# Twelve identity products on TensorE ahead of each wait for a tile's normalised rows

## The chip, the cores and the metric

The kernel runs on one core of one Trainium2 chip. The metric is the device time of one launch in microseconds. Before the change three runs took 3201.06, 3203.36 and 3207.66 us; the median is 3203.36 us.

## The reference, cut to what matters

Two blocks follow one another on a sequence of 256 tokens of width 1024, each with two layers. The change touches only the first block. There, in each layer, the token mixers' outputs are normalised head by head and projected, the result is added to the residual, and the new residual is normalised again for the router and the experts:

```python
y = rms_norm(y.reshape(bn, m, N_GROUPS * h, HEAD_DIM), head_g.reshape(N_GROUPS * h, HEAD_DIM))
y = y * head_scale[:, None]
return y.reshape(bn, m, MIX_W) @ w_out
...
x = x + g1 * y_lat
x = x + g2 * expert_choice_ffn(rms_norm(x, norm2_g[l]) * (1.0 + sc2) + sh2,
                               router_w[l], exp_w_gate[l], exp_w_up[l], exp_w_down[l])
```

All data are float32. The first layer also carries 256 context tokens through the same steps; the second carries the latent tokens alone.

## The kernel before

Tokens lie in tiles of 128 rows. The first layer of the first block has four tiles (two of latents, two of context), the second has two: six tiles in all. Everything is laid out by hand, with semaphores between the engines and eight PSUM banks. Each bank use is a unit with a number, and units belong to lanes: banks 0 and 1 are the DENSE lane, 2 to 5 and 6 to 7 serve the attention. `bank_for(lane)` takes the next unit of a lane and, from the ninth use on, waits until that bank's previous content has been read.

In the middle of each layer two programs are interleaved step by step on every engine: `attend()`, which works through the attention jobs of all tiles (scores L921, turned weights L302, values L943), and `fill()`, which does the dense work and ends with `out_tile(t)` for each tile. A table written out by hand says how many steps of `fill()` stand behind each step of `attend()`. What `attend()` does not cover is run alone, so the last tile of each layer has no other work beside it.

`out_tile(t)` on TensorE is a chain through three engines:

1. It waits for `xn_ready`: VectorE squares and sums the tile's mixed rows (L2231, L2232), ScalarE takes the roots (L1430), VectorE the reciprocals (L2235) and the scaled rows (L2239).
2. It turns the 128 x 1024 rows with eight transposes (helper `turn`, L302, 128x128 float32 products against the identity) into two DENSE banks, from which VectorE and ScalarE copy them to `HT`.
3. It multiplies them by the two halves of `w_out` (L981, 32 products of 128x512).
4. VectorE adds the result to the residual (L2256, L2257), ScalarE squares and takes the root (L1474, L1430), VectorE writes the normalised rows (L2261). TensorE waits for that, the second `xn_ready` of the tile.
5. It turns these rows with eight transposes, VectorE (L2265) and ScalarE scale them into `HT`, and TensorE makes the router's logits (L1004, 16 products of 128x16).
6. VectorE and ScalarE make the softmax, and VectorE goes on to the squares of the next tile.

Behind a wait of TensorE stands everything that TensorE has still to do, the attention's steps too. After the last tile come the routing, the gathering of the experts' tokens (L1116) and the loop over the 16 experts (L781), whose weights stream in through a ring of slots: SyncE issues a load (L505) each time a product of TensorE frees a slot.

The lines around the two waits are these:

```python
nc.tensor.wait_ge(sem["xn_ready"], pe.due("xn_ready"))
for j in range(2):
    u = bank_for(DENSE)
    for k in range(4):
        last = turn(U(u)[:, k * P:(k + 1) * P], XN[:, t, (4 * j + k) * P:(4 * j + k + 1) * P])
    last.then_inc(full[u % BANKS], 1)
```

Of the kernel before, what the change touches and what calls it, by code (L numbers as in the profile page):

```python
# [14 lines left out]
P = 128  # L15
# [16 lines left out]
CN = 512  # L32
RING = 6
BANKS = 8
RING_2 = 4
SLOTS_2 = (2, 3, 0, 1)
PRE_SLOTS = [(0, 1, 2, 3), (3, 0, 1, 2)]
EXPERT_SLOTS = [(4, 5, 3, 0, 1, 2), (4, 5, 2, 3, 0, 1)]
PRE_CHUNKS = 19
ALL = tuple(range(BANKS))  # L40
DENSE, RULE, SIDE = (0, 1), (2, 3, 4, 5), (6, 7)
# [18 lines left out]
class Count:  # L60


    def __init__(self, name, eng):
        self.name, self.eng, self.per_turn = name, eng, {}
        self.base, self.local = Counter(), Counter()
        self.turn = None
        self.nth, self.taken = list(range(BANKS)), Counter()

# [8 lines left out]
    def unit(self, k=1, lane=ALL):  # L77

        for _ in range(k):
            b = lane[self.taken[lane] % len(lane)]  # L80
            self.taken[lane] += 1
            n = self.nth[b]
            self.nth[b] += BANKS
        return n

    def uses(self, n):

        v = n // BANKS + 1
        return v if self.turn is None else self.turn * (self.per_turn["unit"] // BANKS) + v

# [115 lines left out]
def build(nc, A, out, gate_scratch, band):  # L206
    with ExitStack() as ctx:
        ring = ctx.enter_context(nc.sbuf_tensor("ring", [P, RING * KT * CN], F32))
        arena = ctx.enter_context(nc.sbuf_tensor("arena", [P, ARENA], F32))
        bank = [ctx.enter_context(nc.psum_tensor(f"bank{b}", [P, CN], F32)) for b in range(BANKS)]  # L210
        names = [f"bank_full{b}" for b in range(BANKS)] + [f"bank_free{b}" for b in range(BANKS)]
# [11 lines left out]
        def view(at, width):  # L223
            return arena[:, at:at + width]

        ident, ones = view(0, 128), view(128, 4)
# [4 lines left out]
        U = lambda n: bank[n % BANKS]  # L231
# [28 lines left out]

        X1 = ring[:, RING_2 * KT * CN:RING * KT * CN]
        QKT = [X1[:, 2048 * i:2048 * i + 2048].rearrange("p (b n) -> p b n", b=4) for i in range(2)]
# [34 lines left out]
        mm = nc.tensor.matmul  # L297

        def turn(o, i):

            k = i.shape[0]
            return nc.tensor.transpose(o, i, ident[0:k, 0:k])  # L302
# [126 lines left out]
        def tiles(l):  # L429
            return range(4) if l < DEPTH - 1 else range(2)  # L430
# [51 lines left out]
        def _(eng):  # L482
            count = [0]

            def pre_load(l, *pieces):
# [3 lines left out]
                count[0] += 1  # L489
                if i >= RING_2:  # L490
                    nc.sync.wait_ge(sem["chunk_used"], i - RING_2 + 1)
                elif j == 1:
                    eng.dma_start(X[:, 0:2, :], A["x"][0].rearrange("(t p) n -> p t n", p=P)).then_inc(sem["tokens_in"], 16)
                    eng.dma_start(X[:, 2:4, :], A["ctx"][0].rearrange("(t p) n -> p t n", p=P)).then_inc(sem["tokens_in"], 16)
                    nc.sync.wait_ge(sem["rows_in"], sp.due("rows_in", 16 * 9))
                s = PRE_SLOTS[l][j % RING_2]
                for src, to, n in pieces:
# [39 lines left out]
            def load_2(src, kt=KT, n=CN):  # L537

                q = count[0]
                count[0] += 1  # L540
                s = SLOTS_2[q % RING_2]
                nc.sync.wait_ge(sem["chunk_used"], loaded + q - RING_2 + 1)
                eng.dma_start(slot[s][:, 0:kt, 0:n], src.rearrange("(k p) n -> p k n", p=P)).then_inc(sem[f"chunk{s}"], 16)
# [164 lines left out]
        def next_chunk(slots, parts=1, hold=False):  # L708

            s = slots[chunks[0] % len(slots)]  # L710
            chunks[0] += 1
            nc.tensor.wait_ge(sem[f"chunk{s}"], pe.due(f"chunk{s}", 16 * parts))
            if not hold:
                pending[0] = held[0]
                held[0] = 1
            return s
# [15 lines left out]
        def bank_for(lane=ALL):  # L732

            u = pe.unit(lane=lane)
            if u >= BANKS:
                nc.tensor.wait_ge(free[u % BANKS], pe.uses(u - BANKS))
            return u

        def evacuated(units):

            for n_out in units:
                nc.tensor.wait_ge(free[n_out % BANKS], pe.uses(n_out))
# [59 lines left out]
        def _(eng):  # L802
            for l in range(DEPTH):
# [4 lines left out]
                u = pe.unit()  # L808
# [50 lines left out]
                u = pe.unit()  # L859
# [99 lines left out]

                w_out = {}  # L960

                def out_tile(t):

                    yield
                    turned = []
                    nc.tensor.wait_ge(sem["xn_ready"], pe.due("xn_ready"))
                    for j in range(2):
                        u = bank_for(DENSE)
                        for k in range(4):
                            last = turn(U(u)[:, k * P:(k + 1) * P], XN[:, t, (4 * j + k) * P:(4 * j + k + 1) * P])  # L970
                        last.then_inc(full[u % BANKS], 1)
                        turned.append(u)
                    yield
                    for c in range(2):
                        if t == 0:
                            w_out[c] = slot[next_chunk(PRE_SLOTS[l], hold=c == 1)]
                        u = bank_for(DENSE)
                        for k in range(KT):
                            if c == 0 and k % 4 == 0:
                                evacuated([turned[k // 4]])  # L980
                            last = mm(U(u)[:, :], HT[:, k, t * P:(t + 1) * P], w_out[c][:, k, :],  # L981
                                      start=(k == 0), stop=(k == KT - 1))
                            if pending[0] or (c == 1 and k == 0 and t == tiles(l)[-1]):
                                last.then_inc(sem["chunk_used"], 1)
                                pending[0] = 0
                            if k == KT - 1:
                                last.then_inc(full[u % BANKS], 1)
                            if k % 2:
                                yield
                    yield  # L990
                    nc.tensor.wait_ge(sem["xn_ready"], pe.due("xn_ready"))
                    turned = []
                    for j in range(2):
                        u = bank_for(DENSE)
                        for k in range(4):
                            last = turn(U(u)[:, k * P:(k + 1) * P], XN[:, t, (4 * j + k) * P:(4 * j + k + 1) * P])
                        last.then_inc(full[u % BANKS], 1)
                        turned.append(u)
                    yield
                    u = bank_for(DENSE)  # L1000
                    for k in range(KT):
                        if k % 4 == 0:
                            evacuated([turned[k // 4]])
                        last = mm(U(u)[:, 0:N_EXP], HT[:, k, t * P:(t + 1) * P], RW[:, k, :], start=(k == 0), stop=(k == KT - 1))  # L1004
                    last.then_inc(full[u % BANKS], 1)
                    yield

                def fill():
# [71 lines left out]
                    for t in tiles(l):  # L1080
                        yield from out_tile(t)
# [51 lines left out]
                with pe.loop(4, expert_turn(ns)) as g:  # L1133
                    for e in range(4):
# [11 lines left out]
                        for c in range(2):  # L1146
                            for n_out in (ups[c], ups[2 + c]):
                                nc.tensor.wait_ge(free[n_out % BANKS], pe.uses(n_out))
                            u = pe.unit()
# [20 lines left out]
                for c in range(2):  # L1170
                    for t in tiles(l):
                        s = t // 2
                        u = pe.unit()
# [39 lines left out]
            for l in range(DEPTH):  # L1213
                nc.tensor.wait_ge(sem["smalls2"], pe.due("smalls2", 16 * (15 if l == 0 else 11)))
                u = bank_for()
# [4 lines left out]
                for c in range(2):  # L1220
                    w = next_slot_2()
                    for t in range(2):
                        xt = () if c else turn_tile(t) if l == 0 else normed_tile(t)
                        u = bank_for()
# [4 lines left out]
                u = bank_for()  # L1229
# [6 lines left out]
                u = bank_for()  # L1236
                for r in range(16):
                    last = mm(U(u)[0:8, r // 8 * SEQ:(r // 8 + 1) * SEQ], PICK[:, 7 - r % 8:15 - r % 8], SQ[:, r, :],
                              start=(r % 8 == 0), stop=(r % 8 == 7))
# [3 lines left out]
                u = bank_for()  # L1243
# [144 lines left out]
                for c in range(2):  # L1388
                    w = next_slot_2()
                    for t in range(2):  # L1390
                        u = bank_for()
# [6 lines left out]
                for n in FF_TILES:  # L1398
                    w = next_slot_2()
                    for j in range(0, n, 2):  # L1400
                        u = bank_for()
# [1352 lines left out]
```

## Time and profile before

| | |
|---|---|
| median of three runs | 3203.36 us (3201.06 to 3207.66) |
| the profiled execution, its own time | 3201.78 us |
| its span in the trace | 3200.0 us |
| TensorE busy with matmuls | 2916.9 us, 91% of the span |
| VectorE, ScalarE busy | 908.9 us, 550.2 us |
| mean granted clock of TensorE | 0.946 |

The granted clock is a share of full speed: 1.00 stands for 2.4 GHz and 0.50 for 1.2 GHz; a value between them in a stretch of time means that the clock was at the one level for part of it and at the other for the rest. Times in the rows count from the start of the span.

### The profile page before, as it was taken

How to read it: one execution, taken by the hardware profiler on the slowest of the kernel's cores; microseconds unless marked ns; L12 is line 12 of the kernel's file. 1: busy time of each engine (PE TensorE's matmuls, PEld its weight loads, DVE VectorE, ACT ScalarE, POOL GpSimd, SP SyncE). 2: the span in 40 equal slices, each digit the busy share in tenths (PEclk: the TensorE clock that was granted, in tenths of full speed). 3: DMA queues.
4: the chain of work that ended last, by engine and by line, in shares of the span. 5: the costliest groups of instructions: out<-in, count | busy, mean ns of one | idle time of the engine just before them, and what ended most of it. 6: DMA issues, size and time to landing. Idle time of an engine off the chain costs nothing.

```text
span 3200.0 us, 32009 instructions
## 1 busy us (share of the span) xinstructions
PE 2916.9 (91%) x12620; PEld 1682.0 (53%) x12620; DVE 908.9 (28%) x1838; ACT 550.2 (17%) x1059; POOL 91.3 (3%) x159
## 2 busy tenths in 40 slices
PE   6997689888889987999898999999999999999998
PEld 3554334333335544333333585665784686674883
DVE  2545431111114453101111343452100434343001
ACT  1243311111111241110110113230000113310000
POOL 3000000000001000000000100001000000000000
PEclk9997689999999987998988999999999999999999
DMA  9313129999996333999999542224434432224432
GB/s 283 127 49 125 53 88 410 410 410 410 410 405 198 119 138 132 374 409 410 410 410 407 169 154 71 92 74 139 157 116 167 151 131 79 85 74 161 154 130 81
DMA packets 237359, 669.76 MB, mean 209 GB/s; under 512 B 8064, under 2 KB 18616, under 8 KB 237248
## 3 DMA queue, kind: packets, MB, share of 16 engines
q1 hardware_dynamic: 230432, 653.28, 54.2%
q0 software_dynamic: 6816, 14.94, 2.0%
q8 instruction: 77, 1.26, 0.2%
q14 instruction: 34, 0.28, 0.0%
HBM read 667.09 MB, written 2.90 MB: 209 GB/s over the span
## 4 chain that ended last, share of the span: by engine, by line
PE 75%; DMA 17%; DVE 4%; issue 2%; ACT 1%; POOL 0%; SPq 0%; DVEq 0%; ACTq 0%; POOLq 0%
PE bank L768 31%; DMA ring<-in_exp_w_up_dram 16%; PE bank L781 9%; PE bank L1302 9%; PE bank L1320 5%; PE bank L1154 4%; PE bank L981 3%; PE bank L302 3%; PE bank L1177 1%; PE bank L921 1%; PE bank L1116 1%; PE bank L1032 1%; PE bank L822 1%; PE bank L943 1%; PE bank L1019 1%
## 5 line engine op out<-in xcount | busy, mean ns | idle before, releaser
L781 PE MATMUL bank<-ring,arena 128*64 128x512 f32 (+1 forms) x3072 | 711.0, 616 | 114.0 <-DMA ring<-in_exp_w_up_dram 64.7
L768 PE MATMUL bank<-arena,ring 128*128 128x256 f32 (+1 forms) x2496 | 530.2, 374 | 0.6 <-ACT arena L401 0.6
L781 PEld LDWEIGHTS bank<-ring,arena 128*64 128x64 f32 (+1 forms) x3072 | 217.8, 127 | 581.4 <-issue 470.9
L768 PEld LDWEIGHTS bank<-arena,ring 128*128 128x128 f32 x2496 | 463.9, 190 | 67.2 <-ACT arena L401 1.1
L768 PE MATMUL bank<-ring,arena 128*128 128x512 f32 (+1 forms) x1116 | 468.4, 580 | 3.2 <-DVE arena L2719 1.7
L768 PEld LDWEIGHTS bank<-ring,arena 128*128 128x128 f32 x1116 | 210.8, 190 | 250.4 <-issue 245.8
L1302 PE MATMUL bank<-ring,arena 128*128 128x512 f32 x640 | 297.2, 595 | 0.0
L302 PE MATMUL bank<-arena 128*128 128x128 f32 (+4 forms) x516 | 83.4, 310 | 116.3 <-DVE arena L2239 44.4
L1320 PEld LDWEIGHTS bank<-ring 128*128 128x128 f32 x1248 | 154.0, 192 | 42.0 <-issue 37.3
L2409 DVE COPY arena<-bank 128x512 f32<-128x512 f32 (+1 forms) x64 | 44.0, 688 | 452.0 <-PE bank L781 452.0
L1302 PEld LDWEIGHTS bank<-ring,arena 128*128 128x128 f32 x640 | 112.8, 192 | 93.8 <-issue 93.8
L1320 PE MATMUL bank<-ring 128*128 128x128 f32 x1248 | 155.9, 275 | 2.1 <-DVE ring L2659 2.1
L302 PEld LDWEIGHTS bank<-arena 128*128 128x128 f32 (+4 forms) x516 | 67.6, 162 | 149.8 <-DVE arena L2239 46.0
L1154 PEld LDWEIGHTS bank<-arena 128*128 128x128 f32 (+1 forms) x1024 | 130.0, 208 | 26.4 <-issue 26.4
L2424 DVE TENSOR_TENSOR arena<-bank,arena 32x512 f32 x96 | 65.6, 683 | 269.0 <-ACT arena L1733 264.4
L1154 PE MATMUL bank<-arena 128*128 128x64 f32 (+1 forms) x1024 | 134.3, 291 | 0.0
L981 PE MATMUL bank<-ring,arena 128*128 128x512 f32 x192 | 100.7, 665 | 0.2
L2719 DVE TENSOR_TENSOR arena<-arena,bank 128x512 f32<-128x512 f32 x22 | 15.2, 689 | 285.9 <-PE bank L768 285.9
L1725 ACT ACTIVATE arena<-bank 128x256 f32<-128x256 f32 (+1 forms) x64 | 21.2, 331 | 386.7 <-PE bank L1154 386.7
L1474 ACT ACTIVATE arena<-arena 128x256 f32<-128x256 f32 (+8 forms) x92 | 36.6, 397 | 271.1 <-DVE arena L2444 208.7
L1733 ACT COPY arena<-bank 64x512 f32<-64x512 f32 (+1 forms) x64 | 37.1, 580 | 267.2 <-PE bank L781 237.9
L2667 DVE TENSOR_TENSOR ring<-ring,bank 128x512 f32<-128x512 f32 x88 | 60.5, 687 | 56.4 <-PE bank L1320 55.7
(293 smaller groups left out, 2156.2 us busy)
## 6 DMA issues: line engine op xcount, KB each, us to landing
ring<-in_exp_w_gate_dram SPq DMA_DIRECT2D x64, 2048.0 KB, 23.5
ring<-in_exp_w_up_dram SPq DMA_DIRECT2D x64, 2048.0 KB, 21.2
ring<-in_exp_w_down_dram SPq DMA_DIRECT2D x64, 2048.0 KB, 22.0
ring<-in_w_in_dram SPq DMA_DIRECT2D x42, 2048.0 KB, 7.7
ring<-in_ada_w_dram SPq DMA_DIRECT2D x24, 2048.0 KB, 11.7
ring<-in_w_ffn_up_dram SPq DMA_DIRECT2D x20, 2048.0 KB, 7.9
ring<-in_w_out_dram SPq DMA_DIRECT2D x8, 2048.0 KB, 9.9
ring<-in_w_ffn_down_dram SPq DMA_DIRECT2D x8, 2048.0 KB, 7.9
```

The lines of the kernel that those rows point to most:

```text
L302: return nc.tensor.transpose(o, i, ident[0:k, 0:k])
L768: last = mm(o, lhs(k), rhs(k), start=start and k == 0, stop=stop and k == kt - 1)
L781: last = mm(U(us[c])[g * rows:(g + 1) * rows, :], lhs(k), rhs(i, c), start=(k < 2), stop=(k >= KT - 2))
L981: last = mm(U(u)[:, :], HT[:, k, t * P:(t + 1) * P], w_out[c][:, k, :], start=(k == 0), stop=(k == KT - 1))
L1154: last = mm(U(u)[:, (4 * j + i) * M:(4 * j + i + 1) * M], parts[0:2 * M, c, i * P:(i + 1) * P], FOLD[M], start=True, stop=True)
L1302: last = mm(U(u)[:, :], T[:, k, t * P:(t + 1) * P], w[:, k, :], start=(k == 0), stop=(k == KT - 1))
L1320: last = mm(U(u)[:, i * P:(i + 1) * P], lhs(i), rhs(i), start=True, stop=True)
L1474: act(o, i, func, **more).then_inc(sem[then], 1)
L1733: nc.scalar.copy(DOWN_PART[0:M, :], U(u)[M:2 * M, :]).then_inc(sem["down_part"], 1)
L2409: v.tensor_copy(UP_PARTS[0:2 * M, c, :], U(u)[0:2 * M, :]).then_inc(free[u % BANKS], 1)
L2424: ins = tt(o, U(u)[32 * s:32 * s + 32, :], DOWN_PART[32 * s:32 * s + 32, :], ALU.add)
L2667: frees(tt(flat(T), flat(T), U(u)[:, :], ALU.subtract), u)
```

## The change

TensorE issues twelve products of the identity with itself, 128x128 float32 each, ahead of each of the two waits for `xn_ready` in `out_tile(t)`. They are written to the first 128 columns of the DENSE bank that the first four transposes behind the wait overwrite. Nobody reads them. For that the bank is asked for ahead of the wait and no longer behind it. Nothing changes on any other engine.

```diff
+BUSY_PRODUCTS = 12
...
+                def keep_busy(n_products):
+
+                    u = bank_for(DENSE)
+                    for i in range(n_products):
+                        mm(U(u)[:, 0:P], ident[:, :], ident[:, :], start=True, stop=True)
+                    return u
+
                 def out_tile(t):
 
                     yield
                     turned = []
+                    spare = keep_busy(BUSY_PRODUCTS)
                     nc.tensor.wait_ge(sem["xn_ready"], pe.due("xn_ready"))
                     for j in range(2):
-                        u = bank_for(DENSE)
+                        u = bank_for(DENSE) if j else spare
...
                     yield
+                    spare = keep_busy(BUSY_PRODUCTS)
                     nc.tensor.wait_ge(sem["xn_ready"], pe.due("xn_ready"))
                     turned = []
                     for j in range(2):
-                        u = bank_for(DENSE)
+                        u = bank_for(DENSE) if j else spare
```

## Rows read from the trace of the kernel before

**Rows 1.** The page: TensorE's busy time and its granted clock in 40 slices

```profile
PE 2916.9 (91%) x12620; PEld 1682.0 (53%) x12620; DVE 908.9 (28%) x1838; ACT 550.2 (17%) x1059; POOL 91.3 (3%) x159
...
PEclk9997689999999987998988999999999999999999
```

**Rows 2.** Waits of TensorE over the span: total us, times, longest

```profile
PE bank L302 <- DVE arena L2239: 44.4, 6, 11.0
...
PE bank L302 <- DVE arena L2261: 25.7, 6, 5.2
```

**Rows 3.** The chain that ended last, 230 to 480 us: start, us, what

```profile
416.25 0.77 DVE arena L2261
417.06 0.68 PE bank L302 x4
...
419.17 0.42 DVE arena L2265
419.73 3.58 PE bank L1004 x16
```

**Rows 4.** The timeline of TensorE, turns behind the second wait; brackets: idle before

```profile
288.24 1.83 PE L302 MATMUL bank<-arena 128*128 128x128 f32 x8 [4.00 <-DVE arena L2261]
...
332.32 1.56 PE L302 MATMUL bank<-arena 128*128 128x128 f32 x8 [4.15 <-DVE arena L2261]
...
376.14 1.97 PE L302 MATMUL bank<-arena 128*128 128x128 f32 x8 [5.17 <-DVE arena L2261]
...
417.06 1.10 PE L302 MATMUL bank<-arena 128*128 128x128 f32 x8 [4.11 <-DVE arena L2261]
...
1201.64 1.97 PE L302 MATMUL bank<-arena 128*128 128x128 f32 x8 [4.11 <-DVE arena L2261]
...
1242.99 1.10 PE L302 MATMUL bank<-arena 128*128 128x128 f32 x8 [4.11 <-DVE arena L2261]
```

**Rows 5.** Stretches of 2 us: busy PE, PEld, DVE, ACT, POOL, then granted clock

```profile
250.00:252.00 2.00, 2.00 (x16) 2.00 (x16) 1.70 (x8) 0.00 (x0) 0.00 (x0) 0.72 1.06 407
...
288.00:290.00 2.00, 1.76 (x8) 1.43 (x9) 1.04 (x4) 0.00 (x0) 0.00 (x0) 0.61 0.00 0
...
332.00:334.00 2.00, 1.68 (x10) 1.54 (x11) 1.83 (x6) 1.10 (x4) 0.00 (x0) 0.70 0.00 0
...
372.00:374.00 2.00, 0.00 (x0) 0.00 (x0) 1.10 (x3) 1.61 (x3) 0.00 (x0) 0.94 1.02 422
...
418.00:420.00 2.00, 0.43 (x4) 0.30 (x2) 1.47 (x4) 1.64 (x4) 0.00 (x0) 0.53 0.00 0
...
1198.00:1200.00 2.00, 0.00 (x0) 0.00 (x0) 0.00 (x0) 1.98 (x3) 0.00 (x0) 0.95 0.00 0
...
1244.00:1246.00 2.00, 0.43 (x3) 0.37 (x2) 1.40 (x4) 1.71 (x4) 0.00 (x0) 0.54 0.00 0
```

**Rows 6.** The timeline of TensorE: products at either level of the clock

```profile
225.59 1.16 PE L1060 MATMUL bank<-arena 128*128 128x128 f32 x8
...
248.50 1.95 PE L837 MATMUL bank<-arena 128*128 128x2 f32 x16
...
257.86 1.97 PE L302 MATMUL bank<-arena 128*128 128x128 f32 x8 [5.36 <-DVE arena L2239]
...
260.91 3.77 PE L981 MATMUL bank<-ring,arena 128*128 128x512 f32 x4
...
265.57 1.94 PE L981 MATMUL bank<-ring,arena 128*128 128x512 f32 x4
```

**Rows 7.** The timeline of TensorE: router and sixteen small products at the lower level

```profile
291.22 3.57 PE L1004 MATMUL bank<-arena 128*128 128x16 f32 x16
...
435.12 3.53 PE L837 MATMUL bank<-arena 128*128 128x2 f32 x16
```

**Rows 8.** A stretch of the expert loop (last two columns: DMA share, GB/s)

```profile
480.00:490.00 10.00, 10.00 (x51) 3.71 (x48) 1.34 (x2) 2.45 (x3) 0.23 (x1) 1.00 1.02 414
```

## The prediction

> **What bounds the kernel now.** I read the page first. TensorE is busy for 91% of the span, and its granted clock dips in a few slices, most of them in the first block [rows 1]. The diff touches six tiles of that block, two waits each. The waits of TensorE show what these twelve cost: six for the rows after the heads' norm (released by L2239), 44.4 us together, and six for the rows after the second norm (released by L2261), 25.7 us together [rows 2]. Next the chain that ended last, from 230 to 480 us, because a wait costs time only where it lies on the chain. It does: the chain goes through VectorE's L2261, four transposes on TensorE, VectorE's L2265 and the sixteen router products without a gap [rows 3]. So during each of these waits nothing that TensorE could do brings the rows sooner. What can get shorter is TensorE's own part behind the wait, by running at the upper level of its clock.
>
> Behind this stretch comes the expert loop, where the DMA engines are full at 414 GB/s [rows 8]. Its loads are issued only as TensorE frees ring slots, and the ring is filled well before, so the whole loop starts earlier if the stretch ends earlier. A microsecond won here is a microsecond of the span.
>
> **The products themselves.** 6 tiles x 2 waits x 12 = 144 products with as many weight loads. The nearest row at the upper level is eight products of the same shape in 1.16 us [rows 6], so twelve take at most 12 x 0.145 = 1.7 us; at the lower level eight take 1.97 us [rows 6], so at most 12 x 0.246 = 3.0 us. The shortest of the twelve idle times is 4.00 us [rows 4]. Both prices fit in, whichever clock holds, and everything behind the products on TensorE's queue (the attention's steps too) would have waited for the same semaphore. Cost on the path: 0. Without that cover it would be 1.7 to 3.0 us a place.
>
> **The bank asked for earlier.** Ahead of the second wait the bank is that of the first half of L981, which VectorE empties while the second half is computed; ahead of the first wait it is the bank whose reading the router's products have already waited for, or a fold's of long before. Cost: 0, and bounded by what is left of the wait (4.00 us less 1.7, that is 2.3 us) before it could show at all.
>
> **What the clock gives.** The lower level doubles TensorE's part. Its price by piece: eight transposes 1.97 us against 1.10 [rows 4], so 0.87; four products of L981 3.77 us against 1.94 [rows 6], so 1.83; the sixteen router products take 3.57 us [rows 7] and are cold in all six tiles. Of these no warm row exists; the nearest are sixteen 128x2 products with the same weights' shape, 3.53 us at the lower level [rows 7] and 1.95 at the upper [rows 6], so up to 1.6 us a tile.
>
> When does the clock fall? A mean of 0.61 over the two microseconds from 288 says that it was up for (0.61 - 0.50)/0.50 = 22% of them, so it fell at 288.4. The six rows give 288.4, 332.8, 373.8, 418.1, 1199.8 and 1244.2 [rows 5]. TensorE's work before the pause had ended at the start of the turns less the idle time: 284.2, 328.2, 371.0, 412.9, 1197.5 and 1238.9 [rows 4]. So the clock outlived the end of the work by 4.2, 4.6, 2.8, 5.2, 2.3 and 5.3 us, while the rows came after 4.0 to 5.2. Two tiles found it down (376.14 and 1201.64: 1.97 us), two lost it during the turns (1.83, 1.56), two kept it through them (1.10, 1.10) [rows 4]. The change moves the end of the work 1.7 us or less nearer to the rows, so the same pauses become 2.3 to 3.5 us long, and I expect the fall some 1.5 us later, 3.8 to 6.8 us after the old end of work. It then lies behind most turns. It still lies ahead of most router products, which begin about 7 us after that end (291.22 less 284.2 [rows 4, 7]).
>
> *Turns behind the second wait.* On the chain a warm turn is worth less than 0.87 us, because VectorE takes the first bank after four transposes and the router's products wait for VectorE: 2.67 us from turns to router where warm (417.06 to 419.73 [rows 3]). Two tiles are warm already; two more have VectorE busy with other work then. I take 0.4 us for each of the two others: 0.8 us in all; bounds 0 and 4 x 0.87 = 3.5.
>
> *Router products.* Bounds 0 and 6 x 1.6 = 9.6 us. By the fall times above one in six would be reached by the warm clock as a whole; the turns, now following shortly on the products, may add to it. I take two of six, 3.2 us.
>
> *Turns and first L981 products behind the first wait.* Bounds: 0, and 6 x (0.87 + 1.83) = 16.2 us. Here the pauses are 44.4/6 = 7.4 us on average [rows 2], and the twelve products cover less than half. Moreover the clock is down when they begin: after the cold router products in four tiles, and ahead of the first tile it fell at 250.9 although TensorE was busy for the whole of these two microseconds [rows 5]; before it came the sixteen small products at 248.50 [rows 6]. Work of that kind does not hold the clock, and a pause of 3.7 us or more (5.36 - 1.7) would still follow. I take 0.
>
> The sum is 0 + 0 - 0.8 - 3.2 - 0 = -4.0 us. The profiled execution's own time is 3201.78 us (span 3200.0), 1.6 us under the median of 3203.36. So it would become 3197.8, and the median 3199.4. I predict 3199.4 us.
>
> **A rule of the Trainium skill.** In this trace pauses of 4.0 to 4.15 us left the clock up at the start of the turns in four of five cases and down in one [rows 4]. The Trainium skill, page "TensorE: Matmul & The Clock Gate", section "Why this matters for your kernels", advises to leave no idle gap of more than a few microseconds between bursts of matmuls, or the clock drops to its lower level. By that rule, taken alone, all second waits would now be about short enough and the first ones too long, which is the rival below where the clock lasts: 3193.0 us against the sum's 3199.4.
>
> **Rivals.**
>
> *The clock lasts through the second wait and the router.* For it: the pause shrinks to 2.3 us in most tiles. Against it: router products are narrow, and the clock fell at 250.9 under narrow products without any pause [rows 5]. It would give 0.8 + 9.6 = 10.4 us: 3193.0.
>
> *It lasts through the first waits too.* 10.4 + 16.2 = 26.6 us: 3176.8. It needs the clock to rise during twelve products that begin at the lower level and then to outlive 3.7 us of idleness or more; at 1201.64 it had not outlived 4.11 [rows 4].
>
> *Nothing moves.* The falls scatter by 3 us against the end of the work (2.3 to 5.3 us); they move, but to a place ahead of the narrow products again, and in tiles where VectorE is what the router waits for. Then 3203.4.
>
> *Slower.* The twelve products stand in front of the turns where the rows are ready early. From a pause of less than 1.7 us (3.0 us cold) they delay the chain; all twelve places with no pause at all would cost 12 x 3.0 = 36 us: 3239. Against it: the shortest pause is 4.00 us, and faster L981 products shorten a pause only on TensorE's side, not VectorE's. One place alone could not be measured.
>
> **How the numbers follow.** Chances: 0.52 for the forecast (its own range 3195 to 3203), 0.2 for the clock that lasts through the router, 0.04 for the first waits too, 0.18 for nothing, 0.06 for slower. A measurement of this kernel tells no less than about 0.2%, 6.4 us, from no change: below 3197.0 is faster, above 3209.8 slower. Faster: all of the third case, nearly all of the second and a tenth of the first, 0.04 + 0.18 + 0.06 = 0.28. Slower: 0.06 and a little for the scatter of the runs, 0.07. Same: 0.65. The range takes in the second case with the bound of the turns (10.4 + 2.7 = 13.1 us: 3190) and, upward, nothing gained with the scatter of half the three runs' spread (3.3 us: 3206.7, taken as 3206.5); the third case and the slower one are left out.
>
> **What would show it.** The profile after should have 144 more matmuls and weight loads and no longer time between the L981 end and L2261; the idle time ahead of the turns 1.5 us shorter for L2261 and 1.5 to 3 us shorter for L2239; turns of 1.1 us behind L2261 in at least five tiles; router products of about 2 us in one to three; and turns of 1.97 us with L981 products of 3.8 us behind L2239, as before. The prediction is wrong if the first waits' L981 products are warm, if the router products are warm in all tiles or in none, or if a pause has shrunk to nothing.

## The result

The changed kernel took 3186.18 us (median of four runs, 3183.36 to 3188.21) against 3204.46 us for the kernel before on the same chip (also four runs, 3201.06 to 3207.66; the forecast started from the median of three, 3203.36). The ratio is 0.9943, 95% interval 0.9930 to 0.9956: 18.3 us faster, between 14 and 22. The forecast was 4 us, and 3190 was the lower end of its range.

In the profile's page of the changed kernel the number of TensorE's matmuls is the first thing to read.

```profile
span 3183.5 us, 32573 instructions
...
PE 2961.5 (93%) x12908; PEld 1719.0 (54%) x12908; DVE 909.2 (29%) x1838; ACT 550.7 (17%) x1059; POOL 91.6 (3%) x159
```

It rose from 12620 to 12908 [rows 1], by 288. The change issues 144 products. A float32 product of this kernel is two matmuls in the trace. TensorE is busy 45 us longer, and the span is 16.5 us shorter.

The waits of TensorE over the span, total, times and longest, are those of [rows 2], with the lines moved by ten (L2239 is L2249, L2261 is L2271, L302 is L303):

```profile
PE bank L303 <- DVE arena L2249: 17.2, 6, 5.6
...
PE bank L303 <- DVE arena L2271: 9.3, 6, 2.5
```

The idle time went from 44.4 to 17.2 us and from 25.7 to 9.3 us, 44 us less. The products fill it; VectorE's rows come no sooner for that.

The timeline of TensorE around the first two tiles follows (start, duration, line, matmuls, idle before). L967 are the new products, L990 is L981 of before, and L1014 is L1004, the router.

```profile
252.88 3.75 PE L967 MATMUL bank<-arena 128*128 128x128 f32 x24
258.34 1.09 PE L303 MATMUL bank<-arena 128*128 128x128 f32 x8 [1.71 <-DVE arena L2249]
...
260.00 1.98 PE L990 MATMUL bank<-ring,arena 128*128 128x512 f32 x4
...
281.38 2.90 PE L967 MATMUL bank<-arena 128*128 128x128 f32 x24
285.55 1.09 PE L303 MATMUL bank<-arena 128*128 128x128 f32 x8 [1.27 <-DVE arena L2271]
...
288.21 3.05 PE L1014 MATMUL bank<-arena 128*128 128x16 f32 x16 [0.94 <-DVE arena L2275]
...
293.60 5.49 PE L967 MATMUL bank<-arena 128*128 128x128 f32 x24
299.97 1.10 PE L303 MATMUL bank<-arena 128*128 128x128 f32 x8 [0.88 <-DVE arena L2249]
...
302.28 1.95 PE L990 MATMUL bank<-ring,arena 128*128 128x512 f32 x4 [0.60 <-DVE arena L2254]
```

Three readings, in which warm means at the upper level of the clock and cold at the lower. Twelve products take 2.90 us at the upper level of the clock and 5.49 at the lower. Behind both first waits the turns take 1.1 us instead of 1.97, and the first four L990 matmuls 1.98 and 1.95 instead of 3.77 [rows 6] and 3.17 (the second tile's, in the timeline of before). And at the first of them the products began at the lower level: they took 3.75 us, more than 2.90 and less than 5.49. There the clock came back up while they ran. Stretches of 2 us show it (busy PE, PEld, DVE, ACT, POOL, then the granted clock, DMA share, GB/s):

```profile
252.00:254.00 2.00, 2.00 (x11) 2.00 (x11) 1.87 (x4) 0.00 (x0) 0.00 (x0) 0.50 1.06 388
254.00:256.00 2.00, 2.00 (x17) 2.00 (x16) 0.69 (x1) 1.23 (x1) 0.00 (x0) 0.84 1.04 387
256.00:258.00 2.00, 0.63 (x6) 0.44 (x4) 1.51 (x4) 0.86 (x3) 0.00 (x0) 1.00 1.05 386
```

Where the time was won is read from stretches of the span between the same points of the program in both kernels: the first layer's tiles up to its expert loop, then (not shown as a line) that loop and the next layer's start, the second layer's tiles, its expert loop, the rest. First the kernel before, then the changed one:

```profile
250.30:475.30 225.00, 164.65 (x554) 91.91 (x553) 100.79 (x262) 65.83 (x142) 2.18 (x5) 0.76 0.21 75
...
1155.77:1284.80 129.03, 95.42 (x340) 54.23 (x338) 52.30 (x129) 31.26 (x60) 2.14 (x4) 0.75 0.35 127
1284.80:1764.00 479.20, 439.77 (x2046) 174.25 (x2048) 51.70 (x95) 55.49 (x103) 5.62 (x14) 0.89 1.02 406
1764.00:3200.00 1436.00, 1399.73 (x5914) 968.22 (x5910) 426.10 (x793) 219.08 (x429) 20.71 (x34) 0.99 0.35 121
```

```profile
250.80:464.60 213.80, 178.22 (x744) 109.76 (x743) 100.83 (x262) 65.91 (x142) 2.18 (x5) 0.87 0.21 79
...
1142.74:1264.80 122.06, 102.54 (x438) 64.13 (x436) 52.33 (x129) 31.48 (x60) 2.15 (x4) 0.85 0.37 136
1264.80:1744.00 479.20, 440.21 (x2048) 171.36 (x2048) 52.03 (x95) 55.38 (x103) 5.65 (x14) 0.89 1.02 406
1744.00:3183.00 1439.00, 1403.47 (x5912) 969.59 (x5910) 425.89 (x793) 219.21 (x429) 20.78 (x34) 0.99 0.35 121
```

The first layer's tiles take 11.2 us less and the second's 7.0, together 18.2 us, and the mean granted clock in them rises from 0.76 and 0.75 to 0.87 and 0.85. The second layer's expert loop, with the DMA share at 1.02, fills a stretch of the same length and begins 20 us earlier. The stretch that is not shown is 2.3 us shorter (475.30 to 1155.77 before, 464.60 to 1142.74 after) and the rest is 3 us longer, both in work that the change does not touch.

Within the tiles the starts of the turns divide the gain further. From the turns behind a tile's first wait to those behind its second wait it took 3.2, 1.8, 2.0 and 0.5 us less in the four tiles of the first layer and 4.4 and 1.3 us less in the second's two: 13.2 us. From the turns behind a second wait to those behind the next first wait, or to the first expert matmul, it took 0.8, 1.7, 0.0, 1.2, 0.5 and 0.8 us less: 4.9 us.

### The profile page after: what moved, and what is told of

It is laid out like the page before. It is cut to its first block, busy times and chain, and to the rows that moved or that the text cites. A ratio compares the mean times of both kernels' runs of the same rounds, so it can differ in the third digit from the quotient of the medians.

```text
span 3183.5 us, 32573 instructions
## 1 busy us (share of the span) xinstructions
PE 2961.5 (93%) x12908; PEld 1719.0 (54%) x12908; DVE 909.2 (29%) x1838; ACT 550.7 (17%) x1059; POOL 91.6 (3%) x159
## 4 chain that ended last, share of the span: by engine, by line
PE 75%; DMA 16%; DVE 5%; issue 2%; ACT 1%; POOL 0%; SPq 0%; DVEq 0%; ACTq 0%; POOLq 0%
PE bank L769 31%; DMA ring<-in_exp_w_up_dram 15%; PE bank L782 10%; PE bank L1312 9%; PE bank L1330 5%; PE bank L1164 4%; PE bank L990 3%; PE bank L303 2%; PE bank L1126 1%; PE bank L1042 1%; PE bank L1187 1%; PE bank L922 1%; PE bank L823 1%; PE bank L944 1%; DMA ring<-in_ada_w_dram 1%
## 5 line engine op out<-in xcount | busy, mean ns | idle before, releaser
L782 PE MATMUL bank<-ring,arena 128*64 128x512 f32 (+1 forms) x3072 | 736.8, 637 | 91.6 <-DMA ring<-in_exp_w_up_dram 61.2
L782 PEld LDWEIGHTS bank<-ring,arena 128*64 128x64 f32 (+1 forms) x3072 | 229.4, 131 | 573.4 <-issue 497.4
L303 PE MATMUL bank<-arena 128*128 128x128 f32 (+4 forms) x516 | 77.0, 293 | 74.3 <-DVE arena L2249 17.2
L303 PEld LDWEIGHTS bank<-arena 128*128 128x128 f32 (+4 forms) x516 | 62.2, 153 | 105.2 <-DVE arena L2249 18.6
L990 PE MATMUL bank<-ring,arena 128*128 128x512 f32 x192 | 94.2, 629 | 1.1 <-DVE arena L2254 0.9
```

The source lines that it names most:

```text
L782: last = mm(U(us[c])[g * rows:(g + 1) * rows, :], lhs(k), rhs(i, c), start=(k < 2), stop=(k >= KT - 2))
```

## The experiments

Theory A: the products are twice as long as the prediction had them, so they fill the pauses nearly to the end, and the upper level of the clock is there when the rows come, behind the first waits too. The rivals are B (the bank asked for earlier), C (TensorE only has to be busy, or only for a moment) and D (transposes would not do). Each kernel differs from the changed one as its diff shows. All were timed against the kernel before on the same chip, whose median is given behind "against". The ratio is taken over all the runs and can differ by 0.001 from the quotient of the two medians; a gain in microseconds is that of the ratio. The profile is of one execution.

**The bank alone.**

```diff
-                    spare = keep_busy(BUSY_PRODUCTS)
+                    spare = keep_busy(0)
```

at both waits.

> The bank is asked for ahead of both waits, as in the change, but no product is issued. Theory A (the products fill the pauses and so keep or bring back the upper level of TensorE's clock): nothing of the gain is left, 3203 to 3206 us, L981-type products behind the first waits at 3.7 us for four as before. Rival B (the gain comes from the earlier request of the bank, which takes a semaphore wait out of the way of the turns): most of the 18 us is still there, about 3187 us.

Measured: 3206.91 us against 3205.96, ratio 1.0006 (0.9998 to 1.0015). Nothing is left of the gain. In its profile the waits are those of [rows 2] again:

```profile
PE bank L303 <- DVE arena L2249: 44.8, 6, 11.1
PE bank L303 <- DVE arena L2271: 26.2, 6, 5.3
```

B falls. The earlier request makes no difference that the interval lets through (at most 1 us faster, 5 us slower).

**The first waits alone** (`keep_busy(0)` ahead of the second).

> Twelve products ahead of the first wait (heads' norm) of each tile only. Theory A: this is the larger part, since in the changed kernel the transposes and first projection products behind that wait ran warm in four or five of six tiles, about 2.7 us each: 3190 to 3194 us. The prediction's step that the first waits gain nothing would give 3204 us here.

Measured: 3192.47 us against 3205.96, ratio 0.9965 (0.9954 to 0.9977), 11 us faster (7 to 15). The twelve runs lie far apart, from 3183.50 to 3203.89, and the profiled execution is the fastest of them. This is the step to which the prediction had given nothing. The timeline shows warm turns behind first waits and cold ones behind second waits in one kernel:

```profile
256.46 1.09 PE L303 MATMUL bank<-arena 128*128 128x128 f32 x8 [1.72 <-DVE arena L2249]
...
283.75 1.94 PE L303 MATMUL bank<-arena 128*128 128x128 f32 x8 [4.10 <-DVE arena L2271]
```

**The second waits alone** (`keep_busy(0)` ahead of the first).

> Twelve products ahead of the second wait (second norm) of each tile only. Theory A: turns warm in nearly all tiles and router products partly warm, 4 to 8 us: 3197 to 3200 us. If instead the two sites help each other (the clock at the first wait up because the router's part was warm), the two single-site gains add to clearly less than the 18 us of both.

Measured: 3194.49 us against 3205.96, ratio 0.9969 (0.9958 to 0.9979), 10 us faster (7 to 13), more than the 4 to 8 expected, though the interval reaches into it. The sum of both sites, 21 us, is the whole change's 18 within the intervals. So no effect of one site on the other is measured.

**Six products instead of twelve** (`BUSY_PRODUCTS = 6`).

> Six products at each wait in place of twelve. One product is two matmuls in the trace, so six take 1.4 us warm and 2.7 us cold, the durations that the prediction had put down for twelve. Theory A: with these the prediction's sum should hold, 4 us (2 to 8), so 3197 to 3202 us, and the first waits' projection products stay cold. Rival C (any activity in the pause is enough, its length does not matter): 3186 us as with twelve.

Measured: 3202.39 us against 3205.96, ratio 0.9991 (0.9982 to 1.0000): 3 us faster, at most 6 and perhaps nothing. Here the prediction's durations are real. The timeline of this kernel in the first tile:

```profile
254.91 2.84 PE L967 MATMUL bank<-arena 128*128 128x128 f32 x12
261.16 1.43 PE L303 MATMUL bank<-arena 128*128 128x128 f32 x8 [3.40 <-DVE arena L2249]
...
263.67 3.78 PE L990 MATMUL bank<-ring,arena 128*128 128x512 f32 x4
```

Six cold products leave a pause of 3.40 us, and the clock is lost again before L990. The router products took 3.57 us in all six tiles, while the turns behind second waits were warm in five of six. The expectation of 4 us was met by the number only: 3.2 of these 4 us had been put on router products, and these gained nothing. By the middle values half of the products win a sixth of the time. So it is not enough that TensorE works for part of the pause; it matters how much of the pause is left.

**The same time with narrow products.**

```diff
-                        mm(U(u)[:, 0:P], ident[:, :], ident[:, :], start=True, stop=True)
+                        mm(U(u)[:, 0:2], ident[:, :], ident[:, 0:2], start=True, stop=True)
```

> The twelve products stream 2 columns in place of 128 (weights still 128x128). From the 128x2 products of before (sixteen matmuls in 1.95 us warm, 3.5 cold) twelve products, 24 matmuls, take 2.9 us warm and 5.2 us cold, as long as the wide ones. Theory A in the form that the streamed columns count: no gain, 3203 to 3206 us, clock at the lower level behind the pauses. Rival C (TensorE only has to be busy): 3186 us.

Measured: 3203.43 us against 3207.50, ratio 0.9994 (0.9985 to 1.0003), no difference that the measurement tells. The profiled execution is the slowest of the twelve, 3209.74 us. They fill the same time, and the idle pauses are about as short as in the changed kernel, but the clock goes down under them:

```profile
291.32 3.87 PE L967 MATMUL bank<-arena 128*128 128x2 f32 x24
295.49 1.97 PE L303 MATMUL bank<-arena 128*128 128x128 f32 x8 [0.30 <-DVE arena L2271]
```

A pause of 0.30 us and turns at 1.97 us. The stretches of 2 us, with the granted clock behind the five busy times, show the same at this wait and at the tile's first one, where 24 narrow matmuls ran from 258.36 to 263.28:

```profile
258.00:260.00 2.00, 2.00 (x15) 2.00 (x14) 1.86 (x5) 0.00 (x0) 0.00 (x0) 0.67 1.08 401
260.00:262.00 2.00, 2.00 (x11) 2.00 (x10) 0.92 (x2) 0.97 (x1) 0.00 (x0) 0.50 1.03 383
...
292.00:294.00 2.00, 2.00 (x15) 2.00 (x15) 0.43 (x2) 1.98 (x3) 0.00 (x0) 0.70 0.00 0
294.00:296.00 2.00, 1.70 (x9) 1.62 (x10) 1.14 (x3) 0.74 (x3) 0.00 (x0) 0.50 0.00 0
```

TensorE was busy for the whole of the first three, and the clock fell and stayed down. At the first wait of the changed kernel the wide products had brought it back up. C falls in both forms. That TensorE is shown as busy does not tell that its clock is up.

**Transposes instead of products** (24 times `turn(U(u)[:, 0:P], ident[:, :])` at each wait, one matmul each).

> Twenty-four transposes of the identity, one matmul each, in place of the twelve products of two matmuls each: same count of matmuls and columns, about 2.9 us warm and 5.5 cold. Theory A: same as the change, 3185 to 3188 us. Rival D (the rule that transposes do not count for the clock): no gain, 3204 us.

Measured: 3189.84 us against 3207.50, ratio 0.9954 (0.9940 to 0.9969), 15 us faster; the median lies 2 us above the 3185 to 3188 expected. The trace shows 24 of them beginning at the lower level and ending at the upper one, with warm turns behind a pause of 1.79 us. The Trainium skill, page "TensorE: Matmul & The Clock Gate", section "Part 4: PE-mode transpose", says that the full clock does not engage for transposes, because they do not count as busy in the same way. The 4.34 us and the 15 us of this run differ from that, and the measurement decides.

```profile
255.18 4.34 PE L303 MATMUL bank<-arena 128*128 128x128 f32 x24
261.32 1.10 PE L303 MATMUL bank<-arena 128*128 128x128 f32 x8 [1.79 <-DVE arena L2249]
```

Whether they do quite as much as products is open: the intervals overlap. D falls.

**Twice as many** (24 at each wait).

> Twenty-four products at each wait. They take 5.7 us warm, 11 us cold. Behind the second wait the pause is 4.1 us, so TensorE comes 1.6 us late to the turns in six tiles (10 us); behind the first it is 5.4 to 11 us and the clock comes up while they run, so about 8 us against pauses of 5.4, 6.3, 6.7, 11, 7.5 and 7.5: 0 to 3 us late in four of them. Theory A with the products on the path where they are longer than the pause: the gain is given back, 3190 to 3204 us. If late products cost nothing, 3180.

Measured: 3186.71 us against 3207.50, ratio 0.9939 (0.9924 to 0.9953), the same as with twelve within the intervals, and faster than the 3190 to 3204 expected: the gain was not given back. All six router groups were at the upper level (1.93 to 1.99 us), and the second waits had no idle time left at all:

```profile
325.40 5.62 PE L967 MATMUL bank<-arena 128*128 128x128 f32 x48
...
333.46 1.93 PE L1014 MATMUL bank<-arena 128*128 128x16 f32 x16 [0.96 <-DVE arena L2275]
```

The products are now longer than the pause of 4.1 us. The turns start 5.4 us behind the first product in every tile, where with twelve it was 4.2 to 4.3 us in five tiles and 5.3 in one. In spite of that the router products end about as soon: 10.0, 10.0, 11.1, 9.9, 10.0 and 9.9 us behind the first product, against 9.9, 10.0, 12.7, 9.3, 10.5 and 9.6 us with twelve. In these two profiles what the late turns cost, up to 1.2 us a tile, and what the warmer router gives back about cancel, except in the third tile, where the turns were not late.

**The late turns by themselves** (24 at the second waits, none at the first).

> Only the second waits, with 24 products each, 5.6 us against pauses of 4.1 us in five tiles and 5.3 us in one. Against twelve at the same places (3194.5 us): theory A with lateness priced, 1.3 us late in five tiles and 0.3 in one, 6.8 us lost, and router products at 1.93 us in all six tiles in place of three or four, 3 to 5 us won: 3194 to 3199 us. If late products cost nothing, 3190.

Measured: 3197.41 us against 3205.99, ratio 0.9974 (0.9965 to 0.9983), 8 us faster, where twelve gave 10. The profiled execution is the slowest of the eleven, 3202.53 us. The router products were at 1.93 us in four tiles, 2.49 and 3.57 in the others, against 1.93 in two with twelve. That this did not show as time agrees with a price for late turns. But the difference between the two lies inside their intervals, so the price of a late turn is not measured as time.

**Counts fitted to each pause.**

```diff
 BUSY_PRODUCTS = 12
+FIRST_BUSY = ((18, 14, 22, 30), (22, 20))
...
+                    spare = keep_busy(FIRST_BUSY[l][t])
...
+                    spare = keep_busy(16)
```

> Counts fitted to what the changed kernel left of each pause: 18, 14, 22, 30 at the first waits of the first layer, 22 and 20 in the second, 16 at every second wait. Theory A: the first waits of the third, fourth and last tile get warm too and more router products, 3 to 8 us on top of the change: 3178 to 3184 us. If the clock is already held where it can be, 3186 us.

Measured: 3178.47 us against 3207.50, ratio 0.9920 (0.9904 to 0.9935): 26 us faster than before (21 to 31), and some 7 us faster than with twelve everywhere (0.9920 against 0.9943; the intervals overlap between 0.9930 and 0.9935, so the 7 us are likely and not shown). In its profile all turns are warm, and so is the projection in the last tile of the first layer, whose pause of 11 us twelve products had not covered. In the changed kernel and in this one:

```profile
374.78 5.49 PE L967 MATMUL bank<-arena 128*128 128x128 f32 x24
385.88 1.97 PE L303 MATMUL bank<-arena 128*128 128x128 f32 x8 [5.61 <-DVE arena L2249]
387.94 15.58 PE L990 MATMUL bank<-ring,arena 128*128 128x512 f32 x32
```

```profile
373.42 8.69 PE L968 MATMUL bank<-arena 128*128 128x128 f32 x60
384.32 1.10 PE L304 MATMUL bank<-arena 128*128 128x128 f32 x8 [2.21 <-DVE arena L2250]
385.92 13.97 PE L991 MATMUL bank<-ring,arena 128*128 128x512 f32 x32 [0.51 <-DVE arena L2255]
```

Sixty matmuls begin cold, the clock comes up under them, and it is still up when the rows come: 0.9 us less for the turns and 1.6 less for the projection.

**Fitted, with 20 at the second waits** (`keep_busy(20)` instead of 16).

> The fitted first counts with 20 products at the second waits in place of 16: 4.7 us against pauses of 4.1 us, so 0.5 us late in five tiles, 2.5 us lost, against router products warm in nearly all tiles, 3 to 4 us won. Theory A: within 2 us of the fitted kernel, 3177 to 3181 us, so that about 16 is the flat optimum. Rival: the clock at the router decides, 3174.

Measured: 3180.35 us against 3205.99, ratio 0.9921 (0.9907 to 0.9935), as with 16, inside the expected 3177 to 3181. Between 16 and 20 no difference is measured.

**Fitted, and twelve more ahead of the routing's ranks.**

```diff
-                    nc.tensor.wait_ge(sem["rank_ready"], pe.due("rank_ready"))
-                    u = bank_for(RULE)
+                    u = keep_busy(12 if s == len(streams(l)) - 1 else 0, RULE)
+                    nc.tensor.wait_ge(sem["rank_ready"], pe.due("rank_ready"))
```

> The fitted kernel with twelve further products in the pause of 2.9 us that TensorE spends waiting for the ranks of the last stream's routing, in both layers. Behind it come sixteen narrow folds (3.2 to 3.5 us cold, 1.95 warm) and the first gather products (1.8 us for four more when cold). Theory A: up to 3 us a layer, 3 to 6 us in all under the fitted kernel: 3173 to 3176 us. If the narrow folds let the clock go again ahead of the gather, 1.5 us a layer: 3176.

Measured: 3179.65 us against 3205.99, ratio 0.9918 (0.9905 to 0.9932): no difference from the fitted kernel that these runs can tell, and not the 3173 to 3176 expected. The profile shows what was meant to happen, at the narrow folds behind the pause (L839, 1.95 us instead of the 3.24 of the fitted kernel):

```profile
419.46 2.94 PE L968 MATMUL bank<-arena 128*128 128x128 f32 x24
423.24 0.29 PE L304 MATMUL bank<-arena 16*128 16x16 f32 x2 [0.83 <-DVE arena L2376]
423.46 1.95 PE L839 MATMUL bank<-arena 128*128 128x2 f32 x16
```

From the last tile's turns to the first expert matmul it took 462.2 - 407.0 = 55.2 us in the first layer and 1261.4 - 1222.4 = 39.0 in the second, where the fitted kernel's profile has 461.2 - 404.0 = 57.2 and 1263.1 - 1221.7 = 41.4. So some 4 us of one profiled execution each, part of them in the router ahead of the new products. The medians do not confirm them, and I claim no gain.

## Why the prediction was wrong, point by point

**The step that failed is "The products themselves".** It said that twelve take at most 1.7 us at the upper level and 3.0 at the lower, from eight L1060 matmuls in 1.16 us and from eight transposes in 1.97. In the trace they take 2.84 to 2.90 and 5.49 us. The row counts matmuls, not products: the code makes four products there and the trace has eight matmuls, as it has 32 matmuls for the sixteen products of L981 and 16 for the eight of L1004. (Where the text ahead of the prediction calls these 32 and 16 products, it counts matmuls too.) Transposes are one matmul each, and so the turns, which were at hand for comparison, did not warn. The run with six products, which has the durations that the prediction believed in, came out 3 us faster (0 to 6), where the prediction's sum was 4. That agreement is partly luck: of the terms, the turns behind second waits came out warm as forecast, but two of six router groups should have been warm and none was. For the change itself the amount of work that was put into the pauses was half of the real one.

**Everything that followed from it.** The prediction left 2.3 us or more of each second pause and 3.7 or more of each first one. The changed kernel leaves 1.3 to 1.4 us in five of the second pauses and 0.9 to 5.6 in the first.

*The first waits* (taken at 0, upper bound 16.2 us) were the term that was most in error: alone they give 11 us (7 to 15), and in the profile of the changed kernel 13.2 us lie behind them. The clock was down when the products began, as the reason given there has it, but what it drew from that was wrong: in the first tile the clock came up under them (from 0.50 to 1.00 between 252 and 258 us), and the pause that followed was 1.71 us and not 3.7 or more. The second rival, the clock that lasts through the first waits too, was the right mechanism, at a chance of 0.04 and with a price of 26.6 us. The change came in at 18: the fourth tile, with its pause of 11 us, stayed cold behind the first wait, two others were warm there only in part, and the router products were warm in part.

The fitted kernel's 26 us (21 to 31) look like the 26.6 of that rival, but not term by term. Its six router groups still took 16.3 us in all, 5 us less than cold, where the rival had all 9.6; and behind the first waits its profile has 18.0 us less than before, more than the bound of 16.2. That bound priced only the turns and the first four projection matmuls, 2.7 us a tile. The attention's matmuls stand between them and were cold too: in the fifth tile the two scores behind the turns took 2.07 us before and 1.12 in the changed kernel, and the whole stretch became 4.4 us shorter.

*Turns behind the second wait and router products* (0.8 and 3.2 us). In the profile of the changed kernel 4.9 us lie behind the second waits, near these 4.0. The six router groups of the changed kernel take 3.05, 1.93, 3.57, 2.33, 3.57 and 2.63 us: 17.1 us in all instead of 6 x 3.57 = 21.4, so 4.3 us of TensorE's time. Five of six groups of turns are warm. The second waits alone give 10 us (7 to 13), more than these terms. Two things that the sum left out are in its profile: behind the first wait of the second tile, which has no products there, the first four L990 matmuls take 2.03 us instead of the 3.17 of before. The 32 matmuls of the last tile's projection take 14.62 us instead of 16.13. These two places give 2.7 us of its profile that the sum did not have; the clock was up for longer there, though nothing was issued ahead of these waits. The rest of the 10 us is not resolved by place.

**What held.** Cost 0 on the path for the products: with pauses of 4.00 us and more, 2.90 us warm still fitted, and 5.49 us cold came only where the pause was at least 6.3. With 24 products the second pauses were used up, which is the condition of the rival "slower"; the kernel gained no more than with twelve, but it did not become slower. Cost 0 for the bank: the run without products shows none beyond its interval. The second expert loop passing an earlier start on: it begins 20.0 us earlier (1284.8, 1264.8), and the first matmul behind it comes 20.3 us earlier (1766.7, 1746.4). That the clock falls under narrow matmuls: it did so again under those of 2 columns.

**The rule on idle gaps.** With the real durations the pauses that were left are 0.9 to 5.6 us. Turns were fully warm behind nine of them, the longest 3.53 us, cold or nearly so behind 5.61 and behind 2.50 us, and warm only in part behind 2.36. With 2-column products the pauses were as short, and the turns were still at 1.97 us behind all six first waits and three of the second ones. The rule that the prediction took from the Trainium skill, page "TensorE: Matmul & The Clock Gate", section "Why this matters for your kernels", that idle gaps between bursts of matmuls should stay under a few microseconds, was there the first rival's, 3193.0. Applied to the real lengths it points to the measured side; the run with 2-column products shows that it is not the whole of what happens.

## What to carry to other kernels

Before a duration is taken from a row, divide the matmuls of that row by the calls in the code: a float32 product here is two matmuls and a transpose is one. An idle pause of TensorE that lies on the path is room for throwaway products (here 128 columns wide; those of 2 columns gained nothing). Size them to end just ahead of the releasing engine, pause by pause, and count the cold duration where they begin cold; that this gives more than one number for all pauses is likely here and not shown. Their gain is in what runs behind the pause, and where that waits for another engine or is paced by DMA, it is small.

## What the runs showed that I had not expected

Work in the pause not only keeps the clock up, it brings it back: under products that began at the lower level it rose while they ran (24 matmuls in 3.75 us, 60 in 8.69 us where all cold would be 13.7). Under transposes it did the same (24 in 4.34 us). It can also rise just too late for them: in the fourth tile of the changed kernel all 24 ran cold until 380.27 us, and then the granted clock was 0.76 from 380 to 382, 1.00 from 382 to 384 and 0.59 from 384 to 386, while TensorE had nothing to do, and 0.50 again when the turns came at 385.88. Under products of two columns the clock went down, although TensorE was 100% busy. And a loop paced by DMA may not be quite deaf to the clock. From the first expert matmul of the first layer to the first one behind the loop it took 954.9 - 475.3 = 479.6 us before and 945.8 - 464.7 = 481.1 after. Thirty of the last matmuls are these in the two kernels:

```profile
944.79 6.64 PE L781 MATMUL bank<-ring,arena 128*64 128x512 f32 x30
```

```profile
934.00 8.29 PE L782 MATMUL bank<-ring,arena 128*64 128x512 f32 x30
```

In this execution of the changed kernel the clock was down in part of them. One execution each does not tell whether the change has to do with it.
